# One gate group and four mixing-gate groups as quarter products, with the token quarters read back from DRAM

## What is computed

```python
h = rmsnorm(x, norm_g[l])
(a_q, a_ckv, i_q, i_k, i_w, a_gate, b_q, b_k, b_v, b_gate,
 c_q, c_gate, mix_gate) = split_cols(h @ w_in[l], IN_SIZES)
...
# the index scores that choose the keys of attention A
rel = jax.nn.relu(jnp.einsum('bthd,bsd->bths', iqb, ik))
score = jnp.einsum('bths,bth->bts', rel, iwb).astype(jnp.float32)
_, idx = lax.top_k(score, topk)
...
oc = memory_attention(qc, kc, vc) * jax.nn.silu(c_gate)   # oa, ob likewise
g_a, g_b, g_c = jnp.split(jax.nn.sigmoid(mix_gate + gate_bias[l]), N_BRANCH, axis=-1)
merged = g_a * (oa @ w_up_a[l]) + g_b * (ob @ w_up_b[l]) + g_c * (oc @ w_up_c[l])
x = x + merged @ w_o[l]
```

## Time and profile before

| | |
|---|---|
| median of 3 runs | 2502.67 us (2500.9 to 2502.89) |
| the profiled execution | 2501.32 us, of which the span of instructions 2499.6 us |
| mean granted TensorE clock | 0.998 of full speed |
| TensorE (PE) busy | 2481.5 us, 99% |
| VectorE (DVE) busy | 1423.2 us, 57% |
| ScalarE (ACT) busy | 798.6 us, 32% |
| GpSimd (POOL) busy | 624.0 us, 25% |

### The profile page before, as it was taken

One profiled execution on the slowest core, in us unless ns is written; L12 is line 12 of the kernel. 1 busy time (PEld: TensorE's weight loads), 2 busy tenths in 40 slices (PEclk: granted clock), 3 DMA queues, 4 the chain that ended last, 5 costly groups with the idle time before them and its releaser, 6 DMA issues.

```text
span 2499.6 us, 35254 instructions
## 1 busy us (share of the span) xinstructions
PE 2481.5 (99%) x13180; PEld 2078.5 (83%) x13180; DVE 1423.2 (57%) x2381; ACT 798.6 (32%) x1177; POOL 624.0 (25%) x795
## 2 busy tenths in 40 slices
PE   9999999999999999999999999999999999999998
PEld 7788799998888888888888888888888888888886
DVE  5673977973337985545554333555555455455525
ACT  7422444443333432233222122323232222233221
POOL 0213655640011232322000220221222333343100
PEclk9999999999999999999999999999999999999999
DMA  7547233443345676778444453666656545546622
GB/s 276 173 154 198 101 129 125 135 152 118 123 165 187 237 249 221 246 245 288 168 167 151 143 159 121 181 213 195 204 188 202 185 157 165 182 153 205 242 99 101
DMA packets 99959, 443.95 MB, mean 178 GB/s; under 512 B 17622, under 2 KB 17622, under 8 KB 71750
## 3 DMA queue, kind: packets, MB, share of 16 engines
q1 hardware_dynamic: 38712, 241.58, 27.6%
q0 software_dynamic: 61136, 200.86, 25.7%
HBM read 347.27 MB, written 96.59 MB: 178 GB/s over the span
## 4 chain that ended last, share of the span: by engine, by line
PE 96%; DVE 2%; DMA 1%; issue 1%; SPq 0%; POOL 0%; ACT 0%; DVEq 0%; ACTq 0%; POOLq 0%
PE bank L446 24%; PE bank L447 24%; PE bank L448 24%; PE bank L863 10%; PE bank L1214 5%; PE bank L1137 2%; PE bank L1275 2%; PE bank L1116 2%; PE bank L1006 1%; PE bank L982 1%; DMA w_raw<-wst 1%; PE bank L945 1%; DVE t_x L2034 0%; PE bank L1001 0%; PE bank L977 0%
## 5 line engine op out<-in xcount | busy, mean ns | idle before, releaser
L435 DVE TENSOR_TENSOR w_lo<-w_raw,w_hi 128x2048 fp32r<-128x2048 f32 x178 | 409.4, 2300 | 411.5 <-ACT w_hi L430 407.0
L430 ACT ACTIVATE w_hi<-w_raw 128x2048 fp32r<-128x2048 f32 x177 | 338.8, 1914 | 550.2 <-PE bank L448 475.3
L446 PE MATMUL bank<-act_b,w_hi 128*128 128x512 f32 x1280 | 502.2, 392 | 0.0
L447 PE MATMUL bank<-act_b,w_lo 128*128 128x512 f32 x1280 | 499.0, 390 | 0.0
L446 PE MATMUL bank<-act_a,w_hi 128*128 128x512 f32 (+1 forms) x1256 | 494.9, 394 | 4.0 <-DVE w_lo L435 4.0
L448 PE MATMUL bank<-act_b,w_hi 128*128 128x512 f32 x1280 | 498.7, 390 | 0.0
L448 PE MATMUL bank<-act_a,w_hi 128*128 128x512 f32 (+1 forms) x1256 | 490.3, 390 | 0.0
L447 PE MATMUL bank<-act_a,w_lo 128*128 128x512 f32 (+1 forms) x1256 | 490.2, 390 | 0.0
L446 PEld LDWEIGHTS bank<-act_b,w_hi 128*128 128x128 f32 x1280 | 240.4, 188 | 54.4 <-issue 5.2
L446 PEld LDWEIGHTS bank<-act_a,w_hi 128*128 128x128 f32 (+1 forms) x1256 | 236.1, 188 | 55.5 <-issue 5.8
L448 PEld LDWEIGHTS bank<-act_b,w_hi 128*128 128x128 f32 x1280 | 240.4, 188 | 50.2
(11 more groups left out here) (364 smaller groups left out, 2994.8 us busy)
## 6 DMA issues: line engine op xcount, KB each, us to landing
w_raw<-wst SPq DMA_DIRECT2D x210, 1024.0 KB, 5.0
prob_t<-flip_d POOLq DMA_DIRECT2D x64, 512.0 KB, 4.8
flip_d<-flip POOLq DMA_DIRECT2D x56, 512.0 KB, 4.7
mix_d<-stage POOLq DMA_DIRECT2D x24, 512.0 KB, 2.9
mixg<-mix_d POOLq DMA_DIRECT2D x8, 1536.0 KB, 6.8
prob_tk<-flip_d POOLq DMA_DIRECT2D x32, 256.0 KB, 5.7
flip_d<-flip_a POOLq DMA_DIRECT2D x16, 512.0 KB, 2.9
b<-rows_2d POOLq DMA_DIRECT2D x16, 448.0 KB, 10.3
```

Of the source, the lines that this page charges most:

```text
L430: act.activation(w_hi[s][:], w_raw[s][:], ACT.Copy).then_inc(hi_ready, 1)
L435: dve.tensor_tensor(w_lo[s][:], w_raw[s][:], w_hi[s][:].bitcast(F32), ALU.subtract).then_inc(lo_ready, 1)
L446: pe.matmul(out_ap, l_hi, r_hi, start=start, stop=False)
L447: pe.matmul(out_ap, l_lo, r_hi, start=False, stop=False)
```

## The change

1. **Token quarters via DRAM.** VectorE's normed tokens `tr_h`, in four buffers instead of two, are stored to a new DRAM tensor `x_d` (16 stores of 256 KB by GpSimd). Where GpSimd added high and low parts, it now issues four loads of 512 KB for each chunk half, in pieces of 1 KB, straight into the space of `t_x` (`x_raw_q`). VectorE makes the four differences in that space (`x_raw_t`) and splits them. No addition of token quarters is left on GpSimd.
2. **More quarter groups.** `G_S1` is 32 instead of 27: the last gate group (27) and the first four mixing-gate groups (28 to 31) are quarter products. For the latter ScalarE writes tanh of the combined group straight to `stage`.
3. **Index scores.** The eight steps go with four plain groups, 32 to 35, two to a group: one after the first quarter of the group's matmuls, one after the third. The square root of the query norms moves from the first index group to gate group 21.

```diff
-G_S0, G_S1 = G_Q + 2, G_GATE + 7
+G_S0, G_S1 = G_Q + 2, G_MIX + 4
...
+    x_d = nc.dram_tensor("x_d", [KT, P, T], F32).ap()
...
-        tr_h = [sb_at(f"tr_h{i}", [P, T], Y + 20 * KB + 2 * KB * i) for i in range(2)]
+        tr_h = [sb_at(f"tr_h{i}", [P, T], Y + 2 * KB * i) for i in range(4)]
...
-        x_sum = [sb_at(f"x_sum{i}", [P, 4, 256], Y + 12 * KB + 4 * KB * i) for i in range(3)]
         t_x = [[[sb_at(f"t_x{i}{n}{h}", [P, 4, 256], RB + 32 * KB * i + 8 * KB * n + 4 * KB * h, F32R) for h in range(2)]
                 for n in range(4)] for i in range(2)]
+        x_raw_q, x_raw_t = [[[sb_at(f"{name}{i}{n}", [P, 4, 256], RB + 32 * KB * i + 8 * KB * n + 4 * KB * h) for n in range(4)]
+                             for i in range(2)] for h, name in enumerate(("x_raw_q", "x_raw_t"))]
...
-            b0 = 0 if g % 2 else 5
+            b0 = 5 if g % 2 else 0
...
-                wait_read(g - 2)
+                pe.wait_ge(ev_act, g - 2)
+                pe.wait_ge(ev_dve, min(g - 2, G_MIX - 1))
...
-            proj(G_Q + 1, (2, 3), lambda: ssq(0, 0))
+            proj(G_Q + 1, (3, 5), lambda: ssq(0, 0))
...
-            proj(G_S1, (2, 4))
...
-                            pe.wait_ge(*((mix_h, g - G_MIX), (ev_act, g - 1))[n])
+                            pe.wait_ge(*((mix_h, g - G_S1), (ev_act, g - 1))[n])
...
-            def idx_group(i, par):
-                g, t = 2 * i + (G_MIX + par), 2 * i + par
-                first = isinstance(i, int) and i == 0 and par == 0
+            def idx_group(i):
+                g = i + G_S1
+                first = isinstance(i, int) and i == 0
                 if first:
-                    pe.wait_ge(ev_act, G_MIX - 2)
-                    gemm_part(g, 0, act_a, first=True)
-                    pe.wait_ge(ev_dve, G_MIX - 1)
+                    pe.wait_ge(ev_act, G_S1 - 2)
+                gemm_part(g, 0, act_a, first=first)
+                if first:
+                    pe.wait_ge(gc_s, RD0 + G_S1 - G_GATE)
                     pe.wait_ge(rq_s, 1)
-                pe.wait_ge(tl_s, IQ0 + t + 1)
-                idx_units(t, par)
-                for hs in range(1 if first else 0, 4):
-                    gemm_part(g, hs, act_a)
-            for par in range(2):
-                idx_group(0, par)
+                for par in range(2):
+                    pe.wait_ge(tl_s, 2 * i + (IQ0 + par + 1))
+                    idx_units(2 * i + par, par)
+                    gemm_part(g, 2 * par + 1, act_a)
+                    if par == 0:
+                        gemm_part(g, 2, act_a)
+            idx_group(0)
             with pe.Fori(1, 4) as i:
-                for par in range(2):
-                    idx_group(i, par)
...
+                idx_group(i)
...
+                    if g < G_MIX:
+                        act.activation(th_g[:], gate_c[:], ACT.Tanh, scale=0.5).then_inc(ev_act, 1)
+                    else:
+                        act.wait_ge(staged_out[g % 2], 8 * (g - g % 2) - 48)
+                        for n in range(2):
+                            last = act.activation(stage[g % 2][:, n, :], gate_c[:, n, :], ACT.Tanh, scale=0.5,
+                                                  bias=half_b[:, 2 * (g - G_MIX) + n:2 * (g - G_MIX) + n + 1])
+                        last.then_inc(ev_act, 1)
...
             split_hi(act, 2 * G_Q + 1, 1)
-            for n in range(3):
+            for n in range(4):
                 x_sum_hi(0, n)
             split_hi(act, 2 * G_Q + 2, 0)
-            x_sum_hi(0, 3)
+            split_hi(act, 2 * G_Q + 3, 1)
             q_out(0)
-            split_hi(act, 2 * G_Q + 3, 1)
-            act.wait_ge(kst_k, 256)
             for n in range(4):
                 x_sum_hi(1, n)
             part_w_hi(C_S0, range(7))
             q_out(1)
...
+                i = g - G_S1
                 for par in range(2):
-                    g, t = 2 * i + (G_MIX + par), 2 * i + par
+                    t = 2 * i + par
+                    split_hi(act, 2 * g + 1 + par, 1 - par)
...
-                        split_hi(act, 2 * g + (1 + e), 1 - e)
...
-                    mix_out(g, i, par, 0)
-            with act.Fori(0, 3) as i:
-                idx_act(i)
-            idx_act(3, last=True)
+                mix_out(g, g - G_MIX, g % 2)
...
-                if i >= 2:
-                    dve.wait_ge(tt_s, i - 1)
-                    dve.wait_ge(tl_s, i - 1)
-                dve.scalar_tensor_tensor(out=tr_h[i % 2][:], in0=x_raw[:, i, :], scalar=pcol("norm_g", i),
+                if i >= 4:
+                    dve.wait_ge(tt_s, i - 3)
+                    dve.wait_ge(tl_s, i - 3)
+                    dve.wait_ge(x_stored[i % 4], 16 * (i // 4))
+                dve.scalar_tensor_tensor(out=tr_h[i % 4][:], in0=x_raw[:, i, :], scalar=pcol("norm_g", i),
...
-                b11, b12, b22 = x_sum
-                dve.wait_ge(xs_b, X0 + 4 * c + 3)
-                dve.tensor_tensor(b11[:], b12[:], b11[:], ALU.subtract).then_inc(xs_t, 1)
+                (b11, b12, b22, b21), (t1, t3, t2, t4) = x_raw_q[c], x_raw_t[c]
+                dve.wait_ge(xq_loaded[c], 64)
+                dve.tensor_tensor(t1[:], b12[:], b11[:], ALU.subtract).then_inc(xs_t, 1)
+                dve.tensor_tensor(t3[:], b22[:], b12[:], ALU.subtract).then_inc(xs_t, 1)
                 dve.wait_ge(xs_t, X0 + 4 * c + 1)
-                dve.tensor_tensor(b12[:], b22[:], b12[:], ALU.subtract).then_inc(xs_t, 1)
-                dve.wait_ge(xs_t, X0 + 4 * c + 2)
-                dve.tensor_tensor(b22[:], b22[:], b11[:], ALU.subtract).then_inc(xs_t, 1)
-            def x_last_sum(c):
-                dve.wait_ge(xs_b, X0 + 4 * c + 4)
+                if c:
+                    dve.wait_ge(kst_k, 256)
+                dve.tensor_tensor(t2[:], b22[:], t1[:], ALU.subtract).then_inc(xs_t, 1)
                 dve.wait_ge(xs_t, X0 + 4 * c + 3)
-                dve.tensor_tensor(x_sum[0][:], x_sum[2][:], x_sum[0][:], ALU.subtract).then_inc(xs_t, 1)
+                dve.tensor_tensor(t4[:], t2[:], b21[:], ALU.subtract).then_inc(xs_t, 1)
...
             split_lo(dve, 2 * G_Q + 1, 1)
-            dve.wait_ge(kst_v, 256)
-            dve.wait_ge(brow_out, 48)
             x_sums(0)
             mem_keys_out()
+            for n in range(4):
+                x_sum_lo(0, n)
             split_lo(dve, 2 * G_Q + 2, 0)
-            for n in range(3):
-                x_sum_lo(0, n)
-            x_last_sum(0)
-            x_sum_lo(0, 3)
+            split_lo(dve, 2 * G_Q + 3, 1)
             q_out(0)
-            split_lo(dve, 2 * G_Q + 3, 1)
-            dve.wait_ge(kst_k, 256)
             x_sums(1)
-            for n in range(3):
+            for n in range(4):
                 x_sum_lo(1, n)
-            x_last_sum(1)
-            x_sum_lo(1, 3)
             part_w_lo(C_S0, range(7))
             q_out(1)
...
+                    dve.wait_ge(chunk_used, 2 * G_S1 - 1)
+                    dve.memset(score[:], 0.0).then_inc(zero_s, 1)
...
+            for i in range(KT):
+                pool.wait_ge(th_s, i + 1)
+                pool.dma_start(x_d[i], tr_h[i % 4][:]).then_inc(x_stored[i % 4], 16)
...
-            def x_quarter(c, n, k, half):
-                rows, cols = slice(CK * c + 4 * k, CK * c + 4 * k + 4), slice(256 * half, 256 * half + 256)
-                pool.tensor_tensor(x_sum[n][:], act_a[0][:, rows, cols].bitcast(F32), act_a[1][:, rows, cols].bitcast(F32),
-                                   ALU.add).then_inc(xs_b, 1)
...
+                for n, k, half in ((1, 0, 1), (0, 0, 0), (2, 1, 1), (3, 1, 0)):
+                    a = CK * c + 4 * k
+                    pool.dma_start(x_raw_q[c][n][:], x_d[a:a + 4, :, 256 * half:256 * half + 256].rearrange("n p t -> p n t"))\
+                        .then_inc(xq_loaded[c], 16)
...
             pool.wait_ge(kst_v, 256)
             pool.wait_ge(brow_out, 48)
+            for b in range(4):
+                pool.wait_ge(x_stored[b], 64)
             x_quarters(0)
+            pool.wait_ge(kst_k, 192)
+            x_quarters(1)
             bias_rows(rows_n, rpb_in.rearrange("h r c -> h (r c)"))
             pool.wait_ge(sp_o, 8)
             for h in range(HEADS_C):
                 pool.dma_start(k_d[6 + h, :, 0:256], kt_c[:, h, :]).then_inc(kst_k, 16)
-            x_last_quarter(0)
-            x_quarters(1)
             proj_store(G_Q)
...
+            for i in range(3):
                 for par in range(2):
-                    iq_step(i, par)
+                    iq_load(i, par)
+                mix_store(G_S1 + i, i // 2, i % 2, 4)
```

163 lines of the change are left out of this document (67 added, 96 removed).

## The result

The changed kernel takes 2506.16 us (median of 20 runs, 2503.73 to 2507.98), the kernel before 2502.45 us (20 runs, 2500.9 to 2506.5): a ratio of 1.0015, 95% interval 1.0008 to 1.0021. That is 3.7 us slower, under the 5.0 us from which I called a difference a change, and 7.9 us above my 2498.3; it lies 1.2 us outside my range.

A forecast was written before the change was run, and what follows sets the result against it. TensorE, busy 99% of the span, was taken as the bound. Quarter groups 8.05 + group 28's wait 0.4 - pauses 3.3 - token quarters 0.8 = 4.35 us faster: 2496.97, or 2498.3 against the median; range 2489 to 2505.

The forecast's parts named there:

- Five quarter groups, 8.05 us: Groups 27 to 31 as quarter products: each saves 1.61 us, 8.05 us in all, if the feeding engines keep up.
- Three pauses, 3.3 us: Before groups 33, 34 and 35 TensorE waits for the tanh read of bank 0: 1.1 us each, 3.3 us lost.
- rival C: Each of the three pauses is followed by 3.3 us at half clock: 5 us more, 2503.3; chance 0.12.
- the three terms: Quarter groups 27 to 31 save 8.05 us, group 28's vanished weight wait 0.4; pauses before groups 33 to 35 cost 3.3.
- I take nothing for them: Sixteen token stores of 256 KB during token scaling: 38 us at worst, under TensorE's 44 us for the tiles; no cost.
- The landing at 245.0: The four token-quarter loads before chunk 26 land at 245.0, so TensorE waits 8.2 us; this term loses 0.8 us.
- 5.8 MB: Bytes counted from 230 until the token-quarter loads land: 3.7 MB plus 2.1 MB of loads, 14.4 us at 401 GB/s.
- My 3.7 MB up to 240: DMA traffic from 230 to 240 ahead of the token-quarter loads: 2.0 + 1.7 MB, one 1 MB weight chunk included.
- My 13.6 us of VectorE behind the landing: VectorE's sums, memory keys and splits after the loads land take 13.6 us, making chunk 26 ready at 258.6.
- A: Rival: the token-quarter loads land by 241 or sooner; the gain grows to 13.1 us, 2489.6; chance 0.20.
- B: Rival: the 1 KB pieces crawl like the bias table, TensorE waits until 279, loss 20.5 us, 2518.8; no chance stated.
- D: Rival: VectorE bounds the added quarter groups, so the 8.05 us don't come: 2506.4; chance 0.05.

The follow-up runs named there:

- the run without a wait at 120: Changed kernel with the stores of `mem_vn` issued behind the eighth token store, one-row DMAs thereby 3 us earlier: 2500.24 us, kernel before 2502.38.
- the run that held back the second half: Changed kernel with GpSimd waiting until the first four quarter loads landed before issuing the other four and the table: 2502.02 us, kernel before 2502.38.

## Why the prediction was wrong

- **Five quarter groups, 8.05 us: right.** They took 20.16 us each. Group 28's wait is gone too.
- **Three pauses, 3.3 us: right in kind, a little high.** 0.87 us each, 2.6 in all; undone, they gave 2.45 us. The clock stayed at full speed behind them, so rival C is out. From chunk 29 on the three terms together should give 8.05 + 0.4 - 3.3 = 5.15 us; the lag of 12.05 us at chunk 29 has shrunk to 6.75 us at the tanh reads of group 38, 844.13 against 837.38: 5.3 us. With the pauses at 2.6 us the terms make 5.85; where the other 0.5 us went stays open.
- **"I take nothing for them", the token stores: the step that failed.** I asked what the stores do to VectorE and the tiles (one store was late, 1.90 us at 70.2, harmless), and not what stands behind them on GpSimd's queue. I had no row for `first_d` or the stores of `mem_vn`. They moved by 30 us to just ahead of two weight loads, and the lag of 8.2 us before chunk 26 in the profiled execution began there: 5.5 us of waiting and an estimated 2.2 us of half clock are most of it. It is this term that takes the time out of my range; the landing alone would have left it inside. Between them, 8.2 us here and 3.9 us at the token quarters make up the 12.05.
- **The landing at 245.0: mis-sized, by 3.6 us.** In the run without a wait at 120 the first sum starts at 248.59. I counted 5.8 MB; up to there the DMA engines moved 7.0 MB from 230 on, and 6.4 MB in the run that held back the second half, 2.1 of them weights. (My 3.7 MB up to 240 held 1.6 MB of weights, not the one chunk I named.) And the rate fell:

```profile
230.00:235.00 5.00, 5.00 (x24) 4.14 (x23) 2.29 (x1) 0.77 (x1) 3.36 (x5) 1.00 0.98 401
...
245.00:248.60 3.60, 3.60 (x18) 2.98 (x17) 0.01 (x1) 0.00 (x0) 0.00 (x0) 1.00 1.03 349
```

  From 401 to 349 GB/s is 13%, while the pieces of 1 KB moved. In the run that held back the second half only 181 GB/s moved from 245 to the first sum at 249.87, so bytes and rate alone do not give the landing. My 13.6 us of VectorE behind the landing was nearly right (12.96: 248.59 to 261.55). So TensorE waited 10.6 us, not 8.2, and chunk 29 starts at 296.75 there, 4.1 us after before's instead of 0.8: this term is off by 3.3 us. From the end of chunk 25 to chunk 29 my sum has 43.1 us; the execution profiled for the result took 46.1, and the changed kernel on three chips 46.1, 44.7 and 46.6.
- **The sum, corrected.** 5.3 - 4.1 = 1.2 us faster without the delay at 120; timed, that kernel gave 2.1 us (2500.24 against 2502.38). The delay is worth 1.5 us between the medians of one chip (2501.75 against 2500.24, with intervals that overlap), and in the execution profiled for the result 7.6 us: chunk 25 ends at 258.63, against 250.99 with the early stores.
- **Rivals.** A did not occur: nothing landed by 241. Nor did B: the loads took 17 us, not 27 or more. D did not: no wait for a weight part in groups 27 to 31.

**What stays open.** In the measurement of the result all twenty runs of the changed kernel lay at 2503.7 or more; in its repeats on three chips its ratio to before was 0.9998, 0.9994 and 1.0005, each interval including 1, though on the last of them three of eleven runs took 2505.24 us or more. So the 3.7 us of the result did not come back as a median. The profiles differ in the loads behind the one-row DMAs: 18.45 and 20.4 us against 12.7 to 13.4 and 17.1 to 17.7. That these DMAs lengthen the loads is shown, by moving them both ways; why the loads took so much longer in the result was not found, nor why DMAs of 64 bytes hold up other loads. A kernel without these DMAs was not run.
